# Expert rows of a mixture-of-experts layer: added in memory onto two row sets, with weights of four blocks on chip

## What is computed

```python
scores = sigmoid(x @ w_router)                      # (1032, 64)
_, e_idx = top_k(scores + router_bias, 6)
w = take_along_axis(scores, e_idx); w = w / sum(w) * 2.5
for each block of up to 128 rows of one expert e:
    y = (silu(x_rows @ w_gate[e]) * (x_rows @ w_up[e])) @ w_down[e]
routed[token] += w[token, k] * y                    # segment_sum over the 6 chosen experts
y = layer_norm(alpha * x + routed + shared_expert(x), ln2_g, ln2_b)
```

## Time and profile before

| | |
|---|---|
| median of 3 runs | 2388.9 us (2385.74 to 2389.4) |
| profiled execution | 2391.1 us, its span 2389.3 us |
| PE, DVE, ACT, POOL busy | 2299.1, 870.2, 593.0, 340.5 us |
| expert loop, by the chain of waits | from 1538.7 to about 2288 us |
| tail, after it | to 2389.3 us |
| granted TensorE clock, mean | 0.98 |
| memory read, written | 358.35 MB, 49.51 MB |

### The profile page before, as it was taken

The page is one execution under the profiler, slowest core; times in us unless marked ns, Lnnn a source line. Parts: engine busy times, 40 slices in busy tenths (PEclk is TensorE's granted clock), DMA queues, the critical chain, the costliest instruction groups (busy, mean ns, idle before and its releaser), DMA issues.

```text
span 2389.3 us, 27330 instructions
## 1 busy us (share of the span) xinstructions
PE 2299.1 (96%) x9804; PEld 1342.4 (56%) x9804; DVE 870.2 (36%) x1732; ACT 593.0 (25%) x1284; POOL 340.5 (14%) x755
## 2 busy tenths in 40 slices
PE   8998999999999999999999999899999999999986
PEld 6455666667666666666665556454444544545422
DVE  0227888743366662000002558311111111111139
ACT  2126666554244430000001220011111111111111
POOL 0003444202000000000000000122322223222200
PEclk9999999999999999999999999999999999999978
DMA  6211000436411013111103121199999989998866
GB/s 207 103 55 43 2 2 2 170 113 247 118 36 36 24 30 107 44 40 31 36 18 112 62 87 64 59 343 341 352 346 341 352 331 353 351 339 337 312 257 267
DMA packets 126399, 386.48 MB, mean 162 GB/s; under 512 B 20324, under 2 KB 77628, under 8 KB 98000
## 3 DMA queue, kind: packets, MB, share of 16 engines
q1 hardware_dynamic: 104928, 300.88, 34.3%
q0 software_dynamic: 21376, 84.31, 9.6%
HBM read 358.35 MB, written 49.51 MB: 171 GB/s over the span
## 4 chain that ended last, share of the span: by engine, by line
PE 89%; DVE 6%; DMA 2%; issue 1%; ACT 1%; SPq 0%; POOL 0%; DVEq 0%; POOLq 0%; ACTq 0%
PE PS L1101 26%; PE PS L1323 19%; PE PS L1334 9%; PE PS L689 8%; PE PS L802 5%; PE PS L1236 4%; PE PS L835 3%; PE PS L872 3%; PE PS L1220 2%; PE PS L972 2%; PE PS L1275 1%; PE PS L737 1%; PE PS L1394 1%; DVE arena L2340 1%; ACT arena L1405 1%
## 5 line engine op out<-in xcount | busy, mean ns | idle before, releaser
L1101 PE MATMUL PS<-arena 128*128 128x344 f32 x2112 | 615.8, 454 | 3.1 <-ACT arena L1676 3.1
L1101 PEld LDWEIGHTS PS<-arena 128*128 128x128 f32 x2112 | 402.5, 191 | 214.5 <-issue 6.1
L1323 PE MATMUL PS<-arena 128*128 128x512 f32 x1040 | 457.3, 592 | 1.1 <-DVE arena L2288 1.1
L1405 ACT ACTIVATE arena<-PS 128x512 f32<-128x512 f32 (+13 forms) x558 | 264.2, 501 | 657.2 <-PE PS L689 413.4
L689 PEld LDWEIGHTS PS<-arena 128*128 128x128 f32 (+3 forms) x1950 | 235.6, 159 | 190.4 <-issue 127.7
L689 PE MATMUL PS<-arena 128*128 128x128 f32 (+3 forms) x1950 | 289.0, 280 | 33.5 <-DVE arena L1925 8.1
L1323 PEld LDWEIGHTS PS<-arena 128*128 128x128 f32 x1040 | 193.1, 191 | 218.9 <-issue 218.9
L1334 PE MATMUL PS<-arena 128*128 128x512 f32 x520 | 239.2, 593 | 0.7 <-ACT arena L1405 0.7
L2292 DVE TENSOR_TENSOR arena<-PS,arena 128x256 f32<-128x256 f32 x65 | 27.6, 425 | 432.5 <-ACT arena L1726 432.5
L1334 PEld LDWEIGHTS PS<-arena 128*128 128x128 f32 x520 | 94.0, 191 | 94.1 <-issue 94.1
L2374 POOL TENSOR_SCALAR arena<-arena 128x384 f32<-128x384 f32 (+3 forms) x192 | 103.2, 558 | 141.0 <-DVE arena L1902 95.3
(11 more groups left out here) (312 smaller groups left out, 2038.9 us busy)
## 6 DMA issues: line engine op xcount, KB each, us to landing
arena<-in_w_exp_gate SPq DMA_DIRECT2D x65, 1024.0 KB, 6.8
arena<-in_w_exp_up SPq DMA_DIRECT2D x65, 1024.0 KB, 8.9
arena<-in_w_exp_down SPq DMA_DIRECT2D x65, 1024.0 KB, 8.2
arena<-expert_rows SPq DMA_DIRECT2D x8, 3072.0 KB, 12.7
arena<-in_w_in SPq DMA_DIRECT2D x34, 512.0 KB, 3.9
arena<-in_x_prompt SPq DMA_DIRECT2D x16, 512.0 KB, 3.6
arena<-in_w_in SPq DMA_DIRECT2D x16, 256.0 KB, 7.7
arena<-in_win SPq DMA_DIRECT2D x8, 512.0 KB
```

Of the source, the lines that this page charges most:

```text
L1101: ins = mm(PS[:, bank + c, 0:CH], w[:, k, :], rhs[:, k, c * CH:(c + 1) * CH], start=k == 0, stop=k == kts - 1)
L1323: ins = mm(PS[:, 2 + s, :].rearrange("p (h n) -> p h n", h=2), xgT[:, s, k, :], wex[:, :, s, k, :], start=k == 0, stop=k == KT - 1)
L1405: return fn(out, in_, ACT.Copy)
```

## The change

`y_dram` now begins with a table of the routing weights (`wtab`, 8 per token) and holds two sets of 1032 rows. Set 0 is filled with `x1tok` (alpha x plus shared expert) by SP after DVE has made it, set 1 with zeros. Each block's rows are multiplied by their routing weight when they leave PSUM, and the scatter adds them in memory onto set s at row = token. The weights of a block come by a second small indirect DMA on POOL's queue (`weights_in`, 128 x 4 bytes), one turn ahead. PE, SP: the weights of a block (gate, up, down) lie in one of four sets and are counted by one semaphore; the two new sets lie where `x1T` and `x1tok` were. The tail reads both sets (8.5 MB), TensorE adds them with an identity matrix into PSUM (8 matmuls per tile, four tiles of PSUM), DVE takes the statistics from PSUM, ACT applies mean and scale, and DVE multiplies and adds the norm's weights.

```diff
+        up_w = [wex[:, :, 0], wex[:, :, 1], at(4000, 2, KT * DE).rearrange("p h (k n) -> p h k n", k=KT), at(12256, 2, KT * DE).rearrange("p h (k n) -> p h k n", k=KT)]
+        down_w = [wexd[:, 0], wexd[:, 1], at(8096, 2, D), at(16352, 2, D)]
...
+            for w in range(2):
+                gate_up_in(w, w)
+            sp.wait_ge(sem("held"), 4)
+            for t in range(NT):
+                n = rows_of(t)
+                sp.dma_start(acc_rows[1][t * P:t * P + n, :], xg[0:n, 0, :]).then_inc(sem("set_out"), 16)
+            sp.wait_ge(sem("M_done"), NT)
+            sp.dma_start(wtab[0:SEQ * 8, :].rearrange("(t p k) o -> p t (k o)", p=P, k=8), wfin[:, 0:NT - 1, :]).then_inc(sem("set_out"), 16)
...
+            down_in(0, 0)
+            sp.wait_ge(sem("sh_mm"), 4)
+            gate_up_in(2, 2)
+            down_in(2, 2)
...
+            for t in range(NT):
+                sp.wait_ge(sem("acc_done"), t + 1)
+                sp.dma_start(acc_rows[0][t * P:t * P + n, :], x1tok[0:n, t, :]).then_inc(sem("x1_out"), 16)
...
+            sp.wait_ge(sem("x1_out"), 32 * NT)
+            gate_up_in(3, 3)
+            down_in(3, 3)
+            with sp.Fori(1, NE // 4) as q:
+                for p in range(2):
+                    experts = [sp.value_load(blke[0:1, bass.ds(q * 4 + 2 * p + s, 1)], min_val=0, max_val=NE - 1) for s in range(2)]
+                    for s, x in enumerate(experts):
+                        sp.wait_ge(sem(f"gu_mm{s}"), q * 2 + p)
+                        gate_up_in(2 * p + s, x)
+                    for s, x in enumerate(experts):
+                        sp.wait_ge(sem("y_mm"), q * 4 + 2 * p + s - 1)
+                        down_in(2 * p + s, x)
...
-                    pe.wait_ge(sem(f"wex{s}"), 32 * i + 32)
+                    pe.wait_ge(s_set[2 * p + s], 48 * q + 48)
...
-                    pe.wait_ge(sem(f"wexd{s}"), 16 * i + 16)
...
-                copy(ysb[:, s, 512:1024], PS[:, 5 + 2 * s, :]).then_inc(sem("y_ev"), 1)
+                act.wait_ge(sem(f"wg{s}"), 16 * i + 16)
+                fn(ysb[:, s, 512:1024], PS[:, 5 + 2 * s, :], ACT.Copy, scale=wrow[:, s:s + 1]).then_inc(sem("y_ev"), 1)
...
-                V.tensor_copy(ysb[:, s, 0:512], PS[:, 4 + 2 * s, :]).then_inc(sem("y_ev2"), 1)
+                dve.wait_ge(sem(f"wg{s}"), 16 * i + 16)
+                ts(ysb[:, s, 0:512], PS[:, 4 + 2 * s, :], wrow[:, s:s + 1], None, ALU.mult).then_inc(sem("y_ev2"), 1)
...
+                G.tensor_tensor(widx[:, s:s + 1], slotall[:, bass.ds(i * 2 + s + 2, 1)], izero[:, 0:1], ALU.add).then_inc(sem(f"ix{s}"), 1)
...
-                G.indirect_dma_start(out=yrows, out_offset=bass.IndirectOffsetOnAxis(ap=dsts[:, s:s + 1], axis=0),
+                G.indirect_dma_start(out=y_rows, out_offset=bass.IndirectOffsetOnAxis(ap=dsts[:, s:s + 1], axis=0),
                                      in_=ysb[:, s, :], in_offset=None,
+                                     bounds_check=ACC0 + 2 * NTOK - 1, oob_is_err=False, compute_op=ALU.add).then_inc(sem(f"yd{s}"), 16)
+                weights_in(s)
...
+            pool.wait_ge(sem("set_out"), 16 * NT + 32)
...
+            for t in range(NT):
+                if m in Y_IN:
+                    pe.wait_ge(*Y_IN[m])
+                if m >= 4:
+                    pe.wait_ge(sem("normed"), m - 3)
+                for c in range(2):
+                    for k, rows in enumerate((x1tok, other)):
+                        ins = mm(PS[0:n, 2 * (m % 4) + c, :], ident[0:n, 0:n], rows[0:n, t, c * 512:(c + 1) * 512], start=k == 0, stop=k == 1)
+                E.do(ins, sem("summed"))
...
+                stats(PS[0:n, 2 * (m % 4):2 * (m % 4) + 2, :].rearrange("p a b -> p (a b)"), s)
+                if m:
+                    scaled_out(m - 1)
+                dve.wait_ge(sem("std_done"), NT + m + 1)
+                E.step(V.reciprocal(s[:, 15:16], s[:, 14:15]))
+                E.do(stt(s[:, 0:1], s[:, 12:13], -1.0, s[:, 15:16], ALU.mult, ALU.mult), sem("mean_done"))
```

More of the change, by code:

```diff
@@ new lines, in _ @@
+            for (m, (s, _)), hi in zip(Y_IN.items(), list(Y_IN)[1:] + [NT]):
+                for to, rows in ((x1tok, acc_rows[0]), (other, acc_rows[1])):
+                    top = min(hi, NT - 1)
+                    sp.dma_start(to[:, m:top, :], rows[m * P:top * P, :].rearrange("(t p) d -> p t d", p=P)).then_inc(s, 16)
+                    if hi == NT:
+                        sp.dma_start(to[0:BD, NT - 1, :], rows[SEQ:NTOK, :]).then_inc(s, 16)
+            for t in range(NT):
+                m, n = t, rows_of(t)
@@ L1339, in _, with full @@
                 turn_rows(0, s, True)
-            with pe.Fori(0, NE // 2) as i:
+            def full(q, p):
+                i = q * 2 + p
                 for s in range(2):
@@ L1369, in spare @@
                 turn_hidden(i, s)
                 pe.wait_ge(sem("hT_ev"), 2 * i + s + 1)
-                pe.wait_ge(sem(f"wexd{s}"), 16 * i + 16)
                 pe.wait_ge(sem("y_ev"), 2 * i + s + 1)
                 pe.wait_ge(sem("y_ev2"), 2 * i + s + 1)
-                down(s, 0)
-                down(s, 1).then_inc(sem("y_mm"), 1)
+                down(s, w, 0)
+                down(s, w, 1).then_inc(sem("y_mm"), 1)
                 turn_rows(i + 1, s, False)
+            with pe.Fori(0, NE // 4) as q:
+                for p in range(2):
+                    full(q, p)
@@ L2446, in _, with turn, spare @@
+                weights_in(s)
+            def turn(i, first=False):
+                for s in range(2):
+                    rows_in(i + 1, s, i * 3 + 3, False)
+                if first:
+                    pool.wait_ge(sem("x1_out"), 32 * NT)
+                for s in range(2):
+                    rows_out(i, s)
+            def spare(i, s):
+                rows_in(i + 1, s, i * 3 + 3, False)
+                rows_out(i, s)
+            pool.wait_ge(sem("set_out"), 16 * NT + 32)
             for s in range(2):
@@ L2447, in _ @@
                 rows_in(0, s, 1, True)
[L2448 to L2456 removed]
+            for s in range(2):
+                G.tensor_tensor(widx[:, s:s + 1], slotall[:, s:s + 1], izero[:, 0:1], ALU.add).then_inc(sem(f"ix{s}"), 1)
+                pool.wait_ge(sem(f"ix{s}"), 2)
+                weights_in(s)
@@ L2457, in _ @@
+            turn(0, True)
+            with pool.Fori(1, NE // 2) as i:
+                turn(i)
             for lo, hi in SPARE:
```

257 lines of the change are left out of this document (110 added, 147 removed).

## The result

| | before | after |
|---|---|---|
| median | 2388.1 us (4 runs) | 2351.14 us (2348.83 to 2351.57, 4 runs) |
| profiled execution, its span | 2391.1, 2389.3 us | 2348.83, 2346.6 us |
| first gate product to the end of the last down product | 744.6 us | 744.1 us |
| tail, from there to the end of the span | 102.3 us | 62.7 us |
| memory read, written | 358.35, 49.51 MB | 341.48, 58.00 MB |

The ratio is 0.9844, 95% interval 0.9827 to 0.9861: 1.6% faster, clear of the noise. The forecast of 2355 us lies 4 us above the median. The spans differ by 42.7 us. Of these 39.6 came from the tail and 0.5 from the loop.

The account below looks back on a forecast made before the run. The prediction took TensorE alone to bound the loop, with the DMA engines close to full, and DVE to pace the tail. 2391.1 less 33.8 from the tail, loop at no cost, gave 2357.3, as a median 2355; range 2347 to 2389.

Parts of the forecast that it names:

- The loop term of zero: Expert loop: TensorE's matmuls stay the same, a turn stays 22.8 us and no stall is taken.
- The gain in the tail: Tail: 8.5 MB read instead of 24.2 and fewer DVE passes, 33.8 us saved.
- the pair of reads before TensorE: Tail: SP's read of the first tile of both sets, 1 MB, taken as 5.1 us.
- TensorE's start to the third tile's statistics: Tail: TensorE starts at 2297.5, third tile summed at 2316.3, with matmuls at 0.85 us, later 0.44.
- six DVE periods: Tail: DVE as the pace at 4.65 us per tile, bounds 4.5 and 5.0, six times.
- ninth statistics to the end: Tail: from 2344.2, DVE's steps through at 2348.9, ACT 1.1, two DVE passes 2.5, output 3.0, end 2355.5.
- the clock rose some 17 us after the matmuls began: Tail: TensorE again at clock 0.50 for some 17 us; with clock 1.00 from the start, 39.8 us saved at best.
- the POOL term: Loop: POOL's added issues, 1.7 us per slot, move the gathers; of 6.7 us slack 5.0 are left, costing nothing.
- Rival 1: Loop: gathers come late behind adding scatters, TensorE waits 3.1 us a turn, 96 us in all: 2451; chance 0.16.
- The DMA engines: Loop: 8.66 MB a turn at 397 GB/s, 21.8 us, plus 0.6 for small packets: 22.4, under 22.83.
- Rival 2: Loop: DMA engines bound at 353 GB/s, 24.5 us a turn, 33 us lost: 2388, no change; chance 0.09.
- Rival 3: Tail: TensorE stays at 1.2 GHz, nine tiles at 6.8 us, 12 us later: 2367; chance 0.08.

Follow-up runs that it names:

- e9: The changed kernel with the tail taking the 8-row tile first, as the kernel before did, instead of last: 2355.81 us, ratio 0.9865.
- e6: The changed kernel with the tail's last pass (adding the norm's bias) on POOL instead of DVE: 2360.48 us, ratio 0.9887.
- e7: The changed kernel with the tail's last pass on POOL and ten unused matmuls ahead of the tail: 2363.22 us, ratio 0.9897.
- s1: The changed kernel (four weight sets) with one unused 1 MB read added per turn of the expert loop: 2403.62 us, one execution.

## Why the prediction was right, and where not

The forecast of 2355 lies closer to the median than the sum deserved. For the profiled execution the sum has 2357.3 us and 2348.8 were measured: of 8.5 us, 5.8 are the tail's, 2.6 the unchanged stage's, which is luck of the execution, and some 0.1 the rest. The median is 2.3 us above this execution, where before it was 2.2 below, and that hides the other half of it.

**Right.** The loop term of zero: 22.83 us a turn, no transfer late, four sets of no use. The gain in the tail from fewer bytes and fewer DVE passes, with its mechanism. The statistics of 0.69 us from PSUM, the passes of 1.23, the pair of reads before TensorE (4.42 us for 5.1).

**Wrong in size: the tail came out at 62.7 us where the sum had 68.5** (2355.5 less the end of the last down product, 2286.99). Term by term, a minus for what came earlier:

| term | predicted | measured | |
|---|---|---|---|
| last down product to the scatter's issue | 2.1 | 2.4 | +0.3 |
| scatter's issue to TensorE's start | 8.45 | 9.1 | +0.6 |
| TensorE's start to the third tile's statistics | 18.8 | 14.4 | -4.4 |
| six DVE periods | 27.9 | 26.6 | -1.3 |
| ninth statistics to the end | 11.3 | 10.3 | -1.0 |

The step that failed is "the clock rose some 17 us after the matmuls began, and I let it do so again". I carried over the kernel before's 17 us without asking what TensorE did in them: 13.8 went to 16 matmuls of the 8-row tile, and the change had moved that tile to the end, which the sum did not take up. With the old order (e9) this term is 18.2 us (2292.73 to 2310.93) against the 18.8 of the sum. That the whole tail is 68.8 us there, almost the 68.5 worked out, is partly luck: the start of TensorE came 2.0 us later than in the sum and the six periods were 1.4 shorter. The same oversight cost the 0.8 us of output, 32 KB now instead of 512. The DVE period was too high since the two statistics follow each other at 0.61 us (2309.74 to 2310.99 for both, 1.25 and not 1.39), and the four short steps with their gaps take 0.7 and not 0.8.

**Right by less than it looked: the POOL term.** "5.0 us are left" was 1.2. The issue of an adding scatter takes 1.60 us, not 1.02, and the gather lands in 10.7, not 7.4 (8.7 to 11.8 in the other executions). That lies with the add: without it the gather lands in 7.0. Rival 1 named this chain and had its arithmetic right: a scatter of 10.3 us and 4.6 us to the gather behind it, from 1886.2, give 1901.1 for a use at 1902.34, and 1.2 us were left. It decided from a scatter of 12.6 us. The waits of 0.7, 0.2 and 0.2 us on gathers in e9, e6 and e7 show how near it was.

**The DMA engines.** Right in the sum (22.4 us of work in 22.83: a share of 0.98), by two errors that cancel. The work of before was put at 7.88 MB / 397 GB/s = 19.8 us, and its share, 71.9 + 19.7%, is 20.9. The add and the small packets were put at 2.0 and 0.6 us; the shares rose by 6.5 points to 98.1%, 1.5 us. Rival 2 took 353 GB/s as the ceiling for bytes that include the second read; the overloaded loops moved 383 to 387 of such bytes once TensorE waited, and 407 before that. The Trainium skill's 358 GB/s per core (DMA: Bandwidth & Descriptors, where 436 GB/s comes from) is passed by these single-core loops too, with the add's second read counted.

**Rival 3** (TensorE at 1.2 GHz throughout) was wrong: clock 1.00 from about 2301 on. It fell to 0.50 again at about 2328, 2 us before the end of TensorE's matmuls.

## What to carry to other kernels

When a stall or a slow clock of the old trace is carried into a sum, first look by shape at what the engine did in it: a reordered loop may have taken the cause away. Moving a sum into the write pays where fewer bytes are read back and passes vanish, but charge each added row twice on its queue and each adding scatter 0.6 us more of GpSimd, and see whose transfers queue behind it. Before a deeper prefetch is built, check that the shallower one is ever late: here it was not.

## What the runs showed of the hardware that I had not expected

- In a tail that began with 8x8 matmuls TensorE's clock stayed at 0.50 for 13.1 us (e9) and some 17 us (before); with full matmuls from the start it rose after 4.7 to 5.6 us.
- In the loop with an extra megabyte and four sets (s1) waits of 1.9 to 2.5 us were followed, seven times, by some 3.4 us at clock 0.50; nine others of 1.7 to 2.2 us were not.
- A POOL tensor-tensor over 1024 elements (2.34 us) held a DVE scalar-tensor-tensor of a single column for 2.33 us. The Trainium skill (SBUF — State Buffer, who interferes with whom) says that a DVE instruction with two inputs in SBUF contends with a GpSimd instruction that reads it; this instruction has two such inputs, and the trace agrees.
- The add made each 4 KB row cost 0.16 us more of a DMA engine on its queue (0.12 us over both queues), the scatter land in 10.3 us instead of 8.0, and its issue take 1.60 us of POOL instead of 1.02; the bytes that the profile counts don't show it.
